# Hybrid attention and mixture-of-experts step: how the first expert's rows reach TensorE, when the last tile is scaled, and where a root's table is loaded

## What is computed

```
h = rmsnorm(x, g_ffn)                                 # 576 rows of 1024
g_logits = h @ w_group + b_group                      # 4 groups
g_idx = argmax(g_logits)
e_logits = (h @ w_expert + b_expert)[group g_idx]     # 4 experts of the group
top_v, top_i = top_k(softmax(e_logits), 2)
for e in range(16):
    he = silu(h @ w_gate[e]) * (h @ w_up[e])          # 1024 -> 512
    y += combine[:, e] * (he @ w_down[e])             # 512 -> 1024
x = x + y
```

## Time and profile before

| | us |
|---|---|
| median of 3 runs | 1011.21 |
| lowest, highest | 1010.29, 1013.48 |
| the profiled execution | 1012.54 |
| its span, first to last instruction | 1010.4 |
| TensorE busy in it | 990.2 (98%) |
| VectorE busy | 689.5 (68%) |
| ScalarE busy | 509.1 (50%) |
| GpSimd busy | 149.7 (15%) |

### The profile page before, as it was taken

The page is one execution under the profiler, slowest core; times in us unless marked ns, Lnnn a source line. Parts: engine busy times, 40 slices in busy tenths (PEclk is TensorE's granted clock), DMA queues, the critical chain, the costliest instruction groups (busy, mean ns, idle before and its releaser), DMA issues.

```text
span 1010.4 us, 12083 instructions
## 1 busy us (share of the span) xinstructions
PE 990.2 (98%) x4614; PEld 812.8 (80%) x4614; DVE 689.5 (68%) x1003; ACT 509.1 (50%) x680; POOL 149.7 (15%) x184
## 2 busy tenths in 40 slices
PE   9989999999999999999999999999999999999995
PEld 6878888887887888877878888889788888888884
DVE  6699886237656664443448457687889889888893
ACT  6523233335545553332352304554588687887782
POOL 1000001112120301221130000022012122121111
PEclk9999999999999999999999999998999999999998
DMA  9489888882551732553285245137899999999994
GB/s 350 138 250 316 236 222 227 270 247 101 195 192 69 262 114 77 194 204 127 97 299 186 104 152 228 69 127 281 337 401 403 381 404 391 393 405 380 404 397 80
DMA packets 125987, 245.27 MB, mean 243 GB/s; under 512 B 69072, under 2 KB 69376, under 8 KB 113600
## 3 DMA queue, kind: packets, MB, share of 16 engines
q1 hardware_dynamic: 105520, 172.51, 47.1%
q0 software_dynamic: 20112, 71.37, 21.2%
q10 hardware_dynamic: 288, 0.52, 0.1%
HBM read 203.07 MB, written 52.08 MB: 253 GB/s over the span
## 4 chain that ended last, share of the span: by engine, by line
PE 56%; issue 27%; DVE 6%; POOL 3%; SPq 2%; ACT 2%; DMA 1%; POOLq 0%; ACTq 0%; DVEq 0%
PE ps L478 14%; PE ps L480 14%; PE ps L479 14%; PE ps L1861 3%; PE ps L1862 3%; SPq L586 2%; PE ps L1834 2%; POOL x_exp L855 1%; PE ps L1896 1%; POOL out_y L866 1%; PE ps L2004 1%; PE ps L2020 1%; DVE w_lo L450 1%; PE ps L2011 1%; DMA v_tok<-out_v_new 1%
## 5 line engine op out<-in xcount | busy, mean ns | idle before, releaser
L478 PE MATMUL ps<-w_hi,s_hi 128*128 128x512 f32 x640 | 256.4, 401 | 3.1 <-DVE w_lo L414 2.6
L480 PE MATMUL ps<-w_lo,s_hi 128*128 128x512 f32 x640 | 250.3, 391 | 0.0
L479 PE MATMUL ps<-w_hi,s_lo 128*128 128x512 f32 x640 | 249.9, 390 | 0.0
L478 PEld LDWEIGHTS ps<-w_hi,s_hi 128*128 128x128 f32 x640 | 120.6, 188 | 29.2 <-issue 4.6
L479 PEld LDWEIGHTS ps<-w_hi,s_lo 128*128 128x128 f32 x640 | 120.7, 189 | 25.5 <-issue 1.0
L480 PEld LDWEIGHTS ps<-w_lo,s_hi 128*128 128x128 f32 x640 | 120.5, 188 | 25.6
L1013 ACT ACTIVATE stage<-ps,x_rstd 128x512 f32<-128x512 f32 x64 | 43.6, 688 | 150.8 <-PE ps L480 150.4
L414 DVE TENSOR_TENSOR w_lo<-raw,w_hi 128x2048 fp32r<-128x2048 f32 x40 | 91.6, 2290 | 32.2 <-ACT w_hi L409 31.9
L409 ACT CAST w_hi<-raw 128x2048 fp32r<-128x2048 f32 x40 | 76.1, 1908 | 12.0 <-DMA raw<-in_w_in 6.3
L450 DVE TENSOR_TENSOR lo_x<-raw_x,hi_x 128x2048 fp32r<-128x2048 f32 x32 | 72.5, 2286 | 7.9 <-ACT hi_x L427 7.9
L450 DVE TENSOR_TENSOR lo_x<-raw_x,w_hi 128x2048 fp32r<-128x2048 f32 x32 | 72.6, 2286 | 5.4 <-ACT w_hi L427 5.4
(11 more groups left out here) (308 smaller groups left out, 1833.2 us busy)
## 6 DMA issues: line engine op xcount, KB each, us to landing
raw<-in_w_in SPq DMA_DIRECT2D x30, 1024.0 KB, 10.3
raw_x<-in_w_gate SPq DMA_DIRECT2D x30, 1024.0 KB, 24.7
raw_x<-in_w_down SPq DMA_DIRECT2D x18, 1024.0 KB, 24.0
raw_x<-in_w_up SPq DMA_DIRECT2D x16, 1024.0 KB, 21.5
raw<-in_w_up SPq DMA_DIRECT2D x16, 1024.0 KB, 22.4
raw<-in_w_down SPq DMA_DIRECT2D x14, 1024.0 KB, 23.6
x_slots<-in_c_empty SPq DMA_DIRECT2D x4, 2112.0 KB, 11.3
x_exp<-x_slots POOLq DMA_DIRECT2D x16, 528.0 KB, 13.2
```

The lines of the kernel that those rows point to most:

```text
L478: nc.tensor.matmul(out, s_h, w_h, start=first, stop=False)
L479: nc.tensor.matmul(out, s_l, w_h, start=False, stop=False)
L480: return nc.tensor.matmul(out, s_h, w_l, start=False, stop=last)
```

## The change

It does four things. BY_PRODUCT goes from 3 to 2, so that only the last two tiles of ORDER (2 and 3) come by one-hot products, and rows_a now holds what tiles 0, PT and 1 brought; GpSimd therefore reads it behind the third tile's scatters, and holds back the fourth tile's. In `slot_rows` TensorE transposes rows_a instead of multiplying it with the identity, and it comes first in each half of PSUM, which it starts; the products add to it. VectorE scales the last tile's rows behind `choose` instead of ahead of it, the first 512 columns ahead of `place_first` and the others behind it, with a semaphore (last_row) for TensorE. ScalarE takes a root of a constant into an unused column behind the exponentials of the tile before the last, and so has the table loaded there.

```
-BY_PRODUCT = 3
+BY_PRODUCT = 2
...
-    eps = after("eps", [P, 1], f32)
+    eps, spare = after("eps", [P, 1], f32), after("spare", [P, 1], f32)
...
+        own(nc.scalar.activation(spare[:, :], eps[:, :], ACT.Sqrt))
         source_hi(4, ORDER[PT], (1,))
         square_x2(ORDER[PT])
         root_x2(ORDER[PT])
...
-        def rows_of_tile(t):
+        def rows_of_tile(t, c0=0, c1=D_MODEL):
             rows = slice(0, P if t < PT else SAMPLE)
-            v.scalar_tensor_tensor(rows_out[rows, t, 0:D_MODEL], x2[rows, t, :], x2_rms[rows, 1, t:t + 1],
-                                   gffn[rows, :], ALU.mult, ALU.mult)
+            return v.scalar_tensor_tensor(rows_out[rows, t, c0:c1], x2[rows, t, c0:c1], x2_rms[rows, 1, t:t + 1],
+                                          gffn[rows, c0:c1], ALU.mult, ALU.mult)
...
         root_of_tile(ORDER[PT])
-        rows_of_tile(ORDER[PT])
         choose(ORDER[PT])
+        rows_of_tile(ORDER[PT], 0, COLS)
         place_first(ORDER[PT])
+        rows_of_tile(ORDER[PT], COLS).then_inc(last_row, 1)
         place_rows(ORDER[PT])
...
         def placed_rows(n, half):
             t = ORDER[TT - BY_PRODUCT + n]
             pe.wait_ge(onehot_ready, n + 1)
+            if n == BY_PRODUCT - 1 and half:
+                pe.wait_ge(last_row, 1)
             for k in range(4):
                 last = mm(ps[:, half, k * P:(k + 1) * P], rows_out[:, t, rows_of(half, k)], onehot[:, n, :],
-                          start=n == 0 and k == 0, stop=n == BY_PRODUCT - 1 and k == 3)
+                          start=False, stop=n == BY_PRODUCT - 1 and k == 3)
             return last
...
             for k in range(4):
-                mm(ps[:, half, k * P:(k + 1) * P], rows_a[:, rows_of(half, k)], ident, start=False, stop=False)
+                mm(ps[:, half, k * P:(k + 1) * P], rows_a[:, rows_of(half, k)], ident, start=k == 0, stop=False,
+                   is_transpose=True)
...
         source(4, ORDER[PT], x2[:, ORDER[PT], :], (1,))
-        placed_rows(0, 0)
         logits(ORDER[PT], (1,))
-        placed_rows(0, 1)
         for half in range(2):
-            placed_rows(1, half)
+            slot_rows(half)
+            placed_rows(0, half)
         positions(PT)
         for half in range(2):
-            slot_rows(half)
-            placed_rows(2, half).then_inc(x_tr, 1)
+            placed_rows(1, half).then_inc(x_tr, 1)
```

More of the change, by code:

```diff
@@ L343, in build @@
     x_loaded = [sem("x_loaded0"), sem("x_loaded1")]
-    slots_ready, onehot_ready = sem("slots_ready"), sem("onehot_ready")
+    slots_ready, onehot_ready, last_row = sem("slots_ready"), sem("onehot_ready"), sem("last_row")
     sample_kept, rows_a_in = sem("sample_kept"), sem("rows_a_in")
```

## The result

**The changed kernel is slower: a ratio of 1.0041 [1.0022, 1.0060] to the kernel before**, 1016.03 us as the median of six runs (1013.93 to 1018.32) against 1011.86 (1010.29 to 1014.40). The forecast was 1011.0 us and no change, and its range ended at 1012.8. The profiled execution of the changed kernel took 1018.32 us with a span of 1016.4 (before: 1012.54 and 1010.4); it is the longest of its six, so its trace shows more loss than the medians do.

The account below looks back on a forecast made before the run. TensorE sets the pace for eleven experts, then the DMA weight stream. First expert -4.0, given back +1.7 and +2.1, leaves -0.2: 1012.3 against the profiled 1012.54, so median 1011.0 us; range 1008.6 to 1012.8.

Parts of the forecast that it names:

- Table load moved: ScalarE, last routing tile: 1.28 us load hidden behind earlier exponentials; root at 693.3, reciprocal only 0.29 us earlier.
- rows_a landed: Rival, GpSimd's read: landing after 693.9 delays positions; at 11.4 us, end 1014.1, slower; chance 0.08. Forecast landing 692.6.
- The stream had no slack: Rival claimed the weight stream has slack, so TensorE's 2.3 us lead reaches the end: 1008.9; chance 0.2.
- The early table: Rival, ScalarE: a second table reload makes the early load useless; destinations +0.7 us, hidden, 1011.2; chance 0.05.
- TensorE's new wait for rows: Before the second expert: rows land at 715.1, TensorE gets there at 712.6 and waits about 2 us.
- restart: SyncE's weight loads after routing, 715.15 before: bounds -0.6 and 0 us, nearest 0, taken as -0.2.
- the slow start: First expert at a lower clock: the first eight 512-column matmuls could take twice as long, covered by the wait for rows.
- The give-back: Of the first expert's 4.0 us gain, 1.7 lost waiting for rows, 2.1 where the weight stream takes over.
- the end hangs on the restart alone: The end hangs on the weight stream's restart at 715.15, and on TensorE only with what the stream leaves it.
- the TensorE step: Last routing tiles: 7.8 us of products removed, 1.1 us of transposes added; first expert begins at 704.2, 4.0 us earlier.
- 0.6 us earlier: VectorE, last routing tile: with the scaling moved and split, destinations end at 702.45 instead of 703.05.
- that cover: TensorE's positions finish ahead of VectorE's place at 699.45; without this, each microsecond would delay the destinations one for one.

Follow-up runs that it names:

- after_aligned: The changed kernel without its new column, the early root written into a free column of lam: ratio 0.9996 to the kernel before.
- The pair with short scatters: The kernel before and after_aligned, each scatter-adding 16 of 128 rows of every expert's result but the last's: 0.9968 and 0.9961 to the kernel before.
- short_notes: after_aligned, loading again only the 32 columns behind the 1024 of the first expert's rows: ratio 1.0014 to the kernel before.
- aligned_tuned: short_notes plus four useless products in TensorE's gap, and the second expert's rows transposed behind the first expert's fourth block: ratio 1.0005 to the kernel before.
- the two early-block kernels: after_aligned with two weight blocks released before the second expert's rows land, at the last tile's destinations or behind the last scatter: 1.0026 and 1.0021 to the kernel before.
- aligned_filled: after_aligned with four useless products where TensorE stood idle ahead of the second half's logits: ratio 1.0005 to the kernel before.

## Why the prediction was wrong

**The step that failed is the new column.** The part "Table load moved" priced the load, the root, the drain and the Square, and said nothing of where the root's result goes. I read `spare` as a name; it is an address, and with it every large tile moved off its multiple of 128 bytes. This was in the diff, and no cost was put to it, neither nothing nor a bound. Two runs that share no instruction edit show it: the column alone costs 1.0021 and the change without it 0.9996; rounding X up to 128 returns the changed kernel from 1.0041 to 1.0002. The 0.2% of the column and the 0.4% of the whole change overlap in their intervals (1.0009 to 1.0034, 1.0022 to 1.0060), so that the column explains all of it is consistent, not shown to the tenth. The longer fall of the clock (below) isn't what is left over: X rounded up has it too, and stands at 1.0002.

The Trainium skill ("DMA: Bandwidth & Descriptors", "How a descriptor splits into AXI transactions") has a rule for this that should have been weighed: a descriptor that doesn't start at a multiple of 256 bytes begins its first transaction at the boundary below, and the extra bytes take time. The runs agree that the place of a tile costs, and differ in the unit: at 128 bytes off, which is no multiple of 256, they show no cost (1.0001).

**None of the rivals was the one.** rows_a landed 3.9 us after its issue (forecast 4.0) and before it was needed. The stream had no slack. The early table did what it should.

**The steps on the edits held**, as after_aligned shows, measured from the mark (693.25 there): reciprocal 3.34 (forecast 3.39), destinations 11.27 (11.22), first expert's first product 13.08 (12.97), TensorE's new wait for rows 1.37 us (about 2, and 2.5 by the prediction's own 712.6 and 715.1), restart -0.13 us against before (-0.2). The wait is the shorter because the first three blocks took 9.1 us, not 8.4, at a clock that was low at their start: the slow start was covered, as forecast. The lead at the second expert's first product is 2.4 us (27.60 against 30.00; forecast 2.3), and 1.5 at the first SiLU. TensorE in after_aligned:

```profile
695.08 0.29 PE L2061 MATMUL ps<-w_rs,s_hi 128*128 128x40 f32 x1 [1.46 <-DVE s_lo L1303]
696.00 0.75 PE L2118 MATMUL ps<-gen,rows_a 128*128 128x128 f32 x4
...
717.00 1.23 PE L2147 MATMUL ps<-gen,x_exp 128*128 128x128 f32 x8 [1.37 <-DMA x_exp<-x_slots]
...
720.85 0.40 PE L478 MATMUL ps<-hi_x,x_hi 128*128 128x512 f32 x1
```

**The give-back was right in kind and in size.** after_aligned ends at 319.35 from the mark, before at 319.17; ScalarE's waits for weight blocks begin at 836 us instead of 883 and add up to 17.9 instead of 11.2. The pair with short scatters, by one profile each, says that it is the stream that takes the lead. That the end hangs on the restart alone was too strong: short_notes let a block go a little sooner and gained nothing, aligned_tuned ended 1.1 us ahead of it with TensorE's order changed, and the two early-block kernels moved the restart forward by 12.5 and 4.3 us and lost through TensorE. What sets the stream's last microsecond stays open.

**In the TensorE step, the clock was left out.** The prediction counted a slow start of the first expert, but took what stands ahead of it at 0.89 us for the logits, 0.56 us per four transposes and 0.243 us a product record, so 5.9 us from the last logits' first start to positions. In the changed kernel's profile this took 7.13 us (697.50 to 704.63): the logits 1.73, the transposes 0.92 and 0.85, the products 1.85 and 1.78. So logits and transposes were mis-sized, at a clock of 0.50, and the products weren't. The same steps took 6.12 us in after_aligned, where the clock fell later, and 5.66 in aligned_filled, where it didn't. VectorE's two new waits for TensorE, 0.35 and 0.76 us, turned "0.6 us earlier" into 0.5 later (12.29 against 11.82 before; 11.27 in after_aligned, which has neither wait, and 11.17 with the gap filled). The sentence "if that cover were gone, each microsecond would go onto the destinations one for one" held; the price of the cover's going was not worked out. None of this stands out in the time of the whole kernel.

## What to carry to other kernels

An added tile is an added address for all that is placed behind it: compute the base of what follows before and after, and keep it at a multiple of 128 bytes, or put scratch into a tile that is dead at that time. A lead won ahead of a saturated stream is worth what the stream leaves of it, here nothing of 1.5 us; it can be tested by easing the stream and looking whether the lead lasts. And when work is taken out of TensorE's queue, look at what idle time it leaves and at the granted clock behind it, in more than one execution: short transposes and logits took up to twice as long at the lower level.

## What the hardware showed that was not expected

- 32 or 64 bytes of offset of the tiles cost 0.21% and 0.28% of the kernel; at 128 bytes no cost showed, though 119424 is a multiple of 128 and not of 256. The share of the DMA engines in the weight stream reads 1.02 in all cases, so it does not show the loss; the time from first to last SiLU does (264.0 against 265.3 us).
- 1.46 us of idle time ahead of short matmuls was followed by 6 us at 1.2 GHz in the changed kernel and, in after_aligned, by 0.72 on average over the same 6 us. The kernel before, whose TensorE had no gap there, reads 0.72 too: the clock fell amid short products that followed each other without a pause. With the filler it stayed at 1.00. 3.03 us of idle time was followed by 4 us at 0.57 on average; there, 512-column products that follow each other every 0.23 us at full clock stood 0.43 us apart.
- Eight f32 product records of 128 columns took 1.8 to 1.9 us at either level of the clock, where eight logits records of 40 columns took 1.73 and 0.92 us.
- Weight blocks let go beside the last scatters made the last one land some five us later, and beside a load of expert rows took that load from 3.9 us to 8.4.
- A table load for the root held ScalarE for 1.28 us and its root began 1.30 us behind the load's start. The Trainium skill ("ScalarE: Activation LUTs", "What ACT_TABLE_LOAD costs") counts a drain of some 1380 ns besides; the trace shows none.
